# Reordering the side jobs and operand loads of an MLP stage in a fused hybrid block

## The reference

```
h   = modulate(x);  proj = h @ w_in                    # one wide projection
mix = gates * (fourier(proj) @ w_fp, hgrn(proj) @ w_hp) @ w_out + b_out
x   = layernorm(alpha * x + g1 * mix)
h2  = modulate(x)
x   = layernorm(alpha * x + g2 * (square(relu(h2 @ w1 + b1)) @ w2 + b2))    # w1: 1024 x 4096, w2: 4096 x 1024
```

## Time and profile before

| | |
|---|---|
| median of 3 runs | 3273.69 us (3273.14 to 3278.31) |
| the profiled execution | 3274.81 us, of which the span is 3273.0 us |
| mean granted TensorE clock | 0.957 of full speed |
| PE busy | 2954.5 us (90% of the span) |
| DVE busy | 1805.7 us (55%) |
| ACT busy | 1034.5 us (32%) |
| POOL busy | 681.8 us (21%) |
| up stage | 1802.8 us to about 2580 us of the span |
| down stage | from 2580.88 us to the end |

### The profile page before, as it was taken

How to read it: one execution, slowest core, us unless ns; L and a number is a source line. 1 busy time by engine, 2 the same in 40 slices (tenths; PEclk the granted TensorE clock), 3 DMA queues, 4 the chain that set the end, 5 groups by cost and what they waited for, 6 DMA issues and landing times.

```text
span 3273.0 us, 35996 instructions
## 1 busy us (share of the span) xinstructions
PE 2954.5 (90%) x13816; PEld 2425.4 (74%) x13816; DVE 1805.7 (55%) x2454; ACT 1034.5 (32%) x1676; POOL 681.8 (21%) x670
## 2 busy tenths in 40 slices
PE   6999999999996899989999788867999699989994
PEld 3888888888884688868788576756777588868883
DVE  5821133121223888677667666656666555586557
ACT  2421000111113565532112544435454433313330
POOL 0322011000001222112105011110000044464443
PEclk9999999999998999989999899988999899999997
DMA  6732233333325554468747687885766655545542
GB/s 227 256 105 81 78 103 126 107 123 124 103 104 171 160 169 154 126 181 215 229 158 257 235 249 235 251 247 181 222 198 193 209 194 187 212 161 206 194 179 96
DMA packets 332911, 573.00 MB, mean 175 GB/s; under 512 B 23731, under 2 KB 212419, under 8 KB 326726
## 3 DMA queue, kind: packets, MB, share of 16 engines
q1 hardware_dynamic: 256646, 330.00, 31.5%
q0 software_dynamic: 58128, 200.85, 18.2%
q10 hardware_dynamic: 17968, 39.85, 3.6%
HBM read 371.37 MB, written 199.24 MB: 174 GB/s over the span
## 4 chain that ended last, share of the span: by engine, by line
PE 48%; DVE 7%; DMA 6%; issue 3%; ACT 2%; POOL 1%; SPq 0%; ACTq 0%; DVEq 0%; POOLq 0%
PE mix_bank L1553 6%; PE mix_bank L1554 5%; PE mix_bank L1555 5%; PE mix_bank L1515 5%; PE mix_bank L1516 5%; PE mix_bank L1517 5%; PE mix_bank L2323 3%; PE mix_bank L2262 2%; PE mix_bank L130 2%; PE mix_bank L132 2%; PE mix_bank L131 2%; PE mix_bank L1460 1%; PE mix_bank L1461 1%; PE mix_bank L1462 1%; DMA tail_a<-scratch_a 1%
## 5 line engine op out<-in xcount | busy, mean ns | idle before, releaser
L1515 PE MATMUL mix_bank<-tail_oph,tail_wh 128*128 128x512 f32 x896 | 361.5, 403 | 124.1 <-ACT tail_e L1357 94.3
L130 PE MATMUL head_bank<-head_hTh,head_wh 128*128 128x512 f32 x1024 | 401.6, 392 | 2.9 <-DVE head_hTl L547 2.1
L131 PE MATMUL head_bank<-head_hTl,head_wh 128*128 128x512 f32 x1024 | 399.2, 390 | 0.0
L132 PE MATMUL head_bank<-head_hTh,head_wl 128*128 128x512 f32 x1024 | 399.1, 390 | 0.0
L1553 PE MATMUL mix_bank<-tail_oph,tail_ah 128*128 128x512 f32 x896 | 354.2, 395 | 45.4 <-issue 16.5
L1516 PE MATMUL mix_bank<-tail_opl,tail_wh 128*128 128x512 f32 x896 | 358.3, 400 | 0.0
L1517 PE MATMUL mix_bank<-tail_oph,tail_wl 128*128 128x512 f32 x896 | 357.3, 399 | 0.0
L1554 PE MATMUL mix_bank<-tail_opl,tail_ah 128*128 128x512 f32 x896 | 353.2, 394 | 0.0
L1555 PE MATMUL mix_bank<-tail_oph,tail_al 128*128 128x512 f32 x896 | 352.6, 394 | 0.0
L555 DVE CAST head_wh<-head_raw 128x1024 fp32r<-128x1024 f32 x64 | 44.1, 689 | 549.7 <-PE head_bank L132 414.6
L1151 DVE TENSOR_TENSOR tail_al<-tail_a,tail_ah 128x1024 fp32r<-128x1024 f32 x112 | 197.8, 1766 | 230.9 <-ACT tail_ah L1363 230.7
(11 more groups left out here) (275 smaller groups left out, 5548.8 us busy)
## 6 DMA issues: line engine op xcount, KB each, us to landing
tail_a<-scratch_a SPq DMA_DIRECT2D x112, 512.0 KB, 3.2
head_raw<-in_w_in SPq DMA_DIRECT2D x64, 512.0 KB, 4.1
scratch_proj<-head_stage POOLq DMA_DIRECT2D x128, 256.0 KB, 2.7
tail_raw<-in_w SPq DMA_DIRECT2D x64, 512.0 KB, 5.5
scratch_a<-tail_e SPq DMA_DIRECT2D x128, 256.0 KB, 4.9
tail_op<-scratch_w2t SPq DMA_DIRECT2D x28, 1024.0 KB, 5.6
scratch_a<-tail_sm SPq DMA_DIRECT2D x96, 256.0 KB, 8.5
tail_op<-in_w SPq DMA_DIRECT2D x21, 1024.0 KB, 6.0
```

The lines of the kernel that those rows point to most:

```text
L130: nc.tensor.matmul(out, wh, xh, start=(k == 0), stop=False)
L131: nc.tensor.matmul(out, wh, xl, start=False, stop=False)
L132: last = nc.tensor.matmul(out, wl, xh, start=False, stop=(k == k_tiles - 1))
L1515: nc.tensor.matmul(out[:], wh[p % 7][:, k, :], oph[i][:, k, :], start=(k == 0 and i in (0, 1, 3)), stop=False, skip_group_check=True)
```

## The change

Five edits, all in `tail_programs`:

1. The side jobs are in another order: the 16 row jobs first, then the 20 block sums.
2. They have other places (`WORK_AT`): two row jobs in each of the units 2 to 9, one behind product 1 and one behind product 5; one block sum behind product 5 in units 10 to 13; block sums behind products 1 and 5 in unit 14; none in 15 and 16; one behind product 5 in units 17 to 30. No turn has two jobs. The semaphore counts (`steps`, `mix_in`, `keep_left`, `store_left`, `load_row`, `load_mix`) follow.
3. First seam, SP: `load_h(1, 6)` stands ahead of the raw weights of unit 18 and of `store_mixed(15)`.
4. Second seam, SP: `load_a(0)`, `load_a(1)` and `load_w2(0, 0)`, `load_w2(0, 1)` stand ahead of `store_mixed(30)`; `load_a(0)` waits in addition for the stores of the last block sum.
5. Operand splits: `high_op(1, n)` and `low_op(1, n)` come four turns behind the product and not three; `high_op(2, 0)`, `low_op(2, 0)` and `high_op(2, 1)`, `low_op(2, 1)`, which stood behind turn 221, come inside the loop at turns 219 and 221, ahead of the splits of `a`.

```diff
-    WORK = list(range(4, MIX + NTILE))
-    FREE = [u for u in range(1, NU - 1) if u not in (UH - 1, UH)]
-
-    def jobs(u):
-
-        n = FREE.index(u) if u in FREE else None
-        return [] if n is None else WORK[n * len(WORK) // len(FREE):(n + 1) * len(WORK) // len(FREE)]
+    SPLIT = 2
+    WORK = [("row", n) for n in range(NTILE)] + [("mix", q) for q in range(4, MIX)]
+    SLOTS = [(u, i) for u in range(SPLIT, SPLIT + NTILE // 2) for i in (1, 5)] + [(u, 5) for u in range(10, UH - 1)] + [(UH - 2, 1)] + [
+        (u, 5) for u in range(UH + 1, NU - 1)]
+    WORK_AT = dict(zip(sorted(SLOTS), WORK))
+
+    def steps(q):
+        return 4 * q + (2 * NTILE if q >= 4 else 0)
...
             if r == 0:
                 sp.wait_ge(st_left, LEFT0 + 16 * NTILE)
+                sp.wait_ge(*mix_out(MIX - 1))
...
+            if u == UH:
+                sp.wait_ge(up_s, up_at[u - 1, 6] + 1)
+                load_h(1, 6)
             if u + 2 < NU:
                 sp.wait_ge(w_lo, up_at[u, 6] + 1)
                 load_raw(u + 2)
             if seam:
                 sp.wait_ge(up_s, up_at[u, 1] + 1)
                 load_h(1, 1)
+            if u == NU - 1:
+                load_a(0)
+                load_a(1)
+                for i in range(2):
+                    sp.wait_ge(up_s, up_at[u, i] + 1)
+                    load_w2(0, i)
             if u:
                 store_mixed(u - 1)
-            if u == UH:
-                sp.wait_ge(up_s, up_at[u - 1, 6] + 1)
-                load_h(1, 6)
...
             if u == NU - 1:
-                load_a(0)
-                load_a(1)
-                for i in range(4):
+                for i in (2, 3):
                     sp.wait_ge(up_s, up_at[u, i] + 1)
                     load_w2(0, i)
-                    if i in (1, 3):
-                        load_a(2 + i // 3)
+                    load_a(i)
...
-            if (u, i) != (UH - 1, 0) and p - 3 >= 0:
-                w, n = up_order[p - 3]
+            if p >= 4:
+                w, n = up_order[p - 4]
                 if w == UH - 1:
                     low_op(1, n)
...
-            if i == 5:
-                for x in jobs(u):
-                    mix(x) if x < MIX else keep_left(x - MIX)
+            if (u, i) in WORK_AT:
+                kind, n = WORK_AT[u, i]
+                mix(n) if kind == "mix" else keep_left(n)
...
             if p >= SEAM - LOOK2:
+                if p != SEAM - 2:
+                    low_op(2, (p + LOOK2 - SEAM) // 2)
                 low_a(p - (SEAM - LOOK2))
-        low_op(2, 0)
-        low_op(2, 1)
         down_turn(0)
...
             if n == 0:
-                pool.wait_ge(*mix_out(MIX - 1))
+                pool.wait_ge(*mix_out(2))
+                pool.wait_ge(z_s, NTILE)
+                for s in range(2):
+                    pool.wait_ge(st_hf[s], 16 * 4 * 4)
```

More of the change, by code:

```diff
@@ L780, in mix_in @@
     def mix_in(q):
-        return (ld_cm[q % 2], 32 * (q // 2 + 1)) if q < 4 else (ld_cm[0], 32 * (q - 1))
+        return (ld_cm[q % 2], 32 * (q // 2 + 1)) if q < 4 else (ld_cm[0], 64 + 32 + 16 * NTILE + 32 * (q - 3))
     def stored(n):
         return [(st_e[z], 16 * 7 * len(range(z, n, 3))) for z in range(3)]
-    WORK = list(range(4, MIX + NTILE))
-    FREE = [u for u in range(1, NU - 1) if u not in (UH - 1, UH)]
-    def jobs(u):
-        n = FREE.index(u) if u in FREE else None
-        return [] if n is None else WORK[n * len(WORK) // len(FREE):(n + 1) * len(WORK) // len(FREE)]
+    SPLIT = 2
[5 more added lines that the diff above has]
+        return 4 * q + (2 * NTILE if q >= 4 else 0)
     def kept_rows(t, n):
@@ L1136, in mix @@
             nc.vector.tensor_tensor(t[:, 0], b12, b11, ALU.subtract).then_inc(mix_s, 1)
-            dve.wait_ge(mix_s, 4 * q + 1)
+            dve.wait_ge(mix_s, steps(q) + 1)
             nc.vector.tensor_tensor(b12, b22, b12, ALU.subtract).then_inc(mix_s, 1)
             nc.vector.tensor_tensor(t[:, 1], b22, t[:, 0], ALU.subtract).then_inc(mix_s, 1)
-            dve.wait_ge(mix_s, 4 * q + 3)
+            dve.wait_ge(mix_s, steps(q) + 3)
             nc.vector.tensor_tensor(b21, b21, t[:, 1], ALU.subtract).then_inc(mix_s, 1)
         def keep_left(n):
-            dve.wait_ge(ld_cm[0], 32 * (MIX - 2) + 32 + 16 * (n + 1))
+            dve.wait_ge(ld_cm[0], 64 + 32 + 16 * (n + 1))
             nc.vector.tensor_tensor(cm[0][:, 0, :], cm[0][:, 0, :], cm[0][:, 1, :], ALU.mult).then_inc(mix_s, 1)
-            dve.wait_ge(mix_s, 4 * MIX + 2 * n + 1)
+            dve.wait_ge(mix_s, 16 + 2 * n + 1)
             nc.vector.tensor_tensor(cm[0][:, 0, :], cm[0][:, 0, :], ag[:], ALU.add).then_inc(mix_s, 1)
@@ L1417, in up_turn @@
                 high_op(0, 5 + p)
-            if p >= 3:
-                w, n = up_order[p - 3]
+            if p >= 4:
+                w, n = up_order[p - 4]
                 if w == UH - 1:
@@ L1436, in scalar @@
             if p >= SEAM - LOOK2:
+                if p != SEAM - 2:
+                    high_op(2, (p + LOOK2 - SEAM) // 2)
                 high_a(p - (SEAM - LOOK2))
-        high_op(2, 0)
-        high_op(2, 1)
         down_turn(0)
@@ L1586, in load_mix @@
             if q >= 2:
-                pool.wait_ge(*mix_out(q - 2 if q < 5 else q - 1))
+                pool.wait_ge(*(mix_out(q - 2) if q < 4 else (st_left, LEFT0 + 16 * NTILE) if q == 4 else mix_out(q - 1)))
             if q < 8:
@@ L1604, in store_mix @@
             dst = d["h2t"][q // 4, :, :, q % 4] if q < 8 else d["w2t"][(q - 8) // 4, :, :, q % 4]
-            pool.wait_ge(mix_s, 4 * q + 3)
+            pool.wait_ge(mix_s, steps(q) + 3)
             pool.dma_start(dst[0:2].rearrange("o p n -> p o n"), t).then_inc(mix_out(q)[0], 16)
-            pool.wait_ge(mix_s, 4 * q + 4)
+            pool.wait_ge(mix_s, steps(q) + 4)
             pool.dma_start(dst[2:4].rearrange("o p n -> p o n"), cm[b][:].rearrange("p i n -> p (i n)")[:, 512:1536].rearrange("p (o n) -> p o n", o=2)
@@ L1636, in store_left @@
         def store_left(n):
-            pool.wait_ge(mix_s, 4 * MIX + 2 * n + 2)
+            pool.wait_ge(mix_s, 16 + 2 * n + 2)
             pool.dma_start(d["xn1"][n * P:(n + 1) * P, :], cm[0][:, 0, :]).then_inc(st_left, 16)
@@ L1681, in gpsimd @@
                 mix(3)
[L1682 to L1685, removed]
-            else:
-                load_row(x - MIX)
-                store_left(x - MIX)
+        for kind, n in WORK:
+            if kind == "mix":
+                load_mix(n)
+                store_mix(n)
+            else:
+                load_row(n)
+                store_left(n)
         for v in range(1, NV):
```

## The result

The changed kernel takes 3228.71 us (median of 4 runs, 3221.51 to 3232.42), beside 3274.05 us for the one before on the same chip. The ratio is 0.9856 (95% interval 0.9837 to 0.9876): 47 us gained by the ratio and 45 between the medians, where 86 were forecast. The stated range ends at 3228 us: the median lies 0.7 us above it, and 3273.7 us times the ratio, 3226.6 us, lies just inside. The profiled execution took 3232.42 us (span 3230.6), 3.7 us over the median.

A forecast was written before the change was run, and what follows sets the result against it. PE, busy for 90% of the span, was taken as the bound, so time could come only from its pauses. Gains 67.6 - 15 + 23.3 + 10 = 85.9 us took 3273.7 to 3188 us; range 3160 to 3228 us.

The forecast's parts named there:

- part 1: Units 4, 7, 11, 20, 23 and 27: without a second job in a turn DVE doesn't wait; gain 67.6 us.
- part 2: Units 2 to 9, two rows each: DVE comes late at the closely spaced row pairs; cost 15 us, bounds 0 and 52.
- 7 such pairs: Row behind product 5 and the next behind product 1 of unit u+1, two turns apart; first costs 2.7 us.
- each later one costs about 2.05 us: Row pairs after the first: PE's delay lets the next job begin nearer to its product; 6 x 2.05 us.
- no half clock: Row pairs in units 2 to 9: PE's short pauses leave the clock up, as after one earlier 3.36 us pause.
- pairs drop the clock: Rival: each row pair stops PE for 5 us and half clock follows; 52 instead of 15 us, 3225 us; chance 0.15.
- part 3: Unit 14 and first seam: new loss 11 + 17 = 28 us instead of 51.3, gain 23.3 us.
- The sign given for the seam: First seam: the three units from 15 on would take some 75 us.
- The first seam's splits: First seam, seven operands split in ten turns: PE 14.6 us late, with half clock 17 us; bounds 4.5 and 33.
- part 4: Second seam: 12 us lost instead of 24.0, third down product may wait 2 us; gain 10 us, bounds 0 and 20.
- The slower rival: Row chain c in the seven tight gaps outgrows them; slower above c = 16.9 us, 3282 us at 18; chance 0.04.
- The other rivals: Rows hidden and seam short, 3165 us (0.15); seam loads share, not overtake, 3211 us (0.10); no effect, 3274 us (0.02).

The follow-up runs named there:

- e10: e8 with jobs at turns given one by one: rows four or five turns apart, block sums six, none in the first seam; 3223.14 us, ratio 0.9841.
- e11: Changed kernel with SP's seven stores (1.75 MB) held back in units 2 to 9 until the row behind product 5 has landed; 3221.66 us, ratio 0.9833.
- e3: Changed kernel with DVE leaving out the scaling and shifting of all 16 rows, POOL still loading and storing them; 3184.26 us (one run).
- e8: e7 with block sum 4 moved to (1, 5), ahead of the rows, so that unit 14 has one block sum; 3208.18 us, ratio 0.9809.
- e7: Changed kernel with row jobs behind products 4 and 6 instead of 1 and 5; 3218.55 us, ratio 0.9834.
- e6: e5 with block sum 4 moved to (1, 5), so that unit 14 has one job; 3209.64 us, ratio 0.9794.
- e9: e8 with load_h(1, 0), (1, 1), (1, 2) together in SP's unit 15, ahead of raw weights and sums; 3207.95 us, ratio 0.9795.
- e2: Kernel before the change with only the seams' loads and operand splits changed, without the wait of load_a(0); 3258.63 us, ratio 0.9961.
- e12: e10 with block sums seven turns apart and rows three or four turns apart; 3201.22 us, ratio 0.9789.
- e5: Changed kernel with each row job cut into two 256 KB halves using the buffer's halves by turns, behind products 1, 4, 0, 6; 3213.81 us, ratio 0.9808.

## Why the prediction came out as it did

- **The doubles (part 1)** are right to the last digit: the window over units 18 to 30 gives 247.52 us, 13 x 19.04, and DVE waits before the single block sums only once, for 0.80 us. A margin of 1 to 5 us was enough at one job in seven turns; e10, at six turns, shows how near that was, with gaps of up to 19 us between two block sums that end in a wait.
- **The rows (part 2)** are the step that failed. It said "7 such pairs" and "each later one costs about 2.05 us", 15 us, "with no half clock". Its wait of 3.7 us behind product 1 was measured at 3.69 to 3.99 in five of the six units 4 to 9, and at 5.20 in the other. But it counted only one of the two chains of a unit. Product 5 comes five turns behind product 1, 13.6 us, which leaves 11.1 beside the row's own 2.45, and I took for granted that a 7.00 us chain fits in. With the low part behind the row releasing SP's transfers, that chain is 14 to 15 us. DVE then waits twice a unit, PE pauses 4.6 to 5.1 us in five of the seven units instead of 2, and the half clock follows all but one of the pauses: 49.3 us. The inference "no half clock" from a single row of 3.36 us failed with it. This is the rival "pairs drop the clock" in manner and size (52 us, 3225 us, and units of 26 us as its sign); its counter-argument, that SP's raw loads go out behind the row, points at the cause: what SP sends there, the raw weights and above all the seven stores behind them, lands on the row's own store and load. e11 shows that SP's stores make the long chain, e3 that the loss comes through DVE alone, e10 that the rows cost 15 us where both chains have more room.
- **Unit 14 (part 3)** took 11 us for the first job, from a wait of 8.43 us (row below), and "waits little" for the second one. That waited 8.06 us: its chain is 2190.15 - 2172.09 = 18.1 us, again with SP's raw weights (issued at 2172.72) and the stores behind them in it, beside 11.6 us for the first. e8 puts the pair at 95.63 (e7) - 82.38 = 13 us, e6 at 15. The sign given for the seam, 75 us for three units, left out this pair, whose pause falls into unit 15; the sum itself implies 85, and 96.75 were measured.

```profile
2169.34 0.69 DVE L1141 TENSOR_TENSOR all_mod<-tail_cm 128x512 f32<-128x512 f32 x1 [8.43 <-DMA tail_cm<-in_w]
...
2190.15 0.69 DVE L1141 TENSOR_TENSOR all_mod<-tail_cm 128x512 f32<-128x512 f32 x1 [8.06 <-DMA tail_cm<-in_w]
```

- **The first seam's splits (part 3)** were forecast at 17 us; units 16 and 17 lose 12.9 and 10.6 us, 23.5 together. ACT's wait for `load_h(1, 6)`, 12.53 us in the earlier trace rows, is gone as forecast, and what is late next is partly DVE, as said. What I left out is `load_h(1, 2)`: it stays behind `store_mixed`, and ACT waits 4.06 us for it. e9, which moves it, leaves that undecided, so what the remaining loss hangs on stays open.

```profile
2217.74 1.90 ACT L1325 CAST tail_oph<-tail_op 128x2048 fp32r<-128x2048 f32 x1 [4.06 <-DMA tail_op<-scratch_h2t]
```

- **The second seam (part 4)**: forecast 12 us lost and 2 later, measured 7.6 and 4.8: 12.4 us, right in sum, by two errors of 4 and 3 us, which is luck. The later loss was forecast at the third down product, for data that comes late. It is at the fifth one, and not new: PE waits 9.88 us for DVE there, whose list the low parts of the operands fill, and waited 7.93 us in the kernel before (row below). The rest is a pause of 0.71 us and 2.1 us of PE's own time at the lower clock.

```profile
2618.04 0.77 PE L1553 MATMUL mix_bank<-tail_oph,tail_ah 128*128 128x512 f32 x1 [7.93 <-DVE tail_sum L1174]
```

- **The slower rival** needed c = 16.9 us in the tight gaps. The tight chains stayed at 6.8 to 8.3; it was the wide ones that grew, to 14 or 15.
- **The other rivals** fell: the rows were not hidden, and the seams' edits did gain (e2), loads and splits together.

A second buffer for the jobs, which would take the chains apart, was not tried. The causes of part 2 are shown. That the sum of chains gives the 24.5 us units of e7 follows from how chains are measured and is no separate proof. Why e12's rows lose 42 us at 3.8 turns stays open in detail.

## What to carry to other kernels

When jobs share one buffer, list every chain between them round the whole period and not only the shortest gap: where all are waited for, the period is their sum and the jobs' own work. Ask of each job what the instruction right behind it releases, since a burst that it lets go lands on the job's own store and load. A chain measured in a quiet place is its lower bound only; take the price with the neighbours' traffic in it before calling a gap wide enough.

## What the runs showed of the hardware

- A 512 KB row load took 3.3 us with nothing beside it (2007.86 to 2011.20), 3.8 us with 1 MB of raw weights issued 3.9 us earlier (e11), and 9.2 to 10.5 us beside the raw weights and SP's seven stores, 1.75 MB. Moving these stores behind the load took 6 to 7 us off it and its store, and put 3 us on the next row's store.
- The length of a PE pause alone did not decide the clock behind it. In the changed kernel a pause of 2.50 us left it at the upper of its two levels, and one of 2.28 us was followed by the lower one (first matmul 0.76 us). In e5 a pause of 4.16 us still left it at the upper one (0.47 us), while in the changed kernel all of 4.57 us and more were followed by the lower. e10's units 4 to 10, with six pauses of 0.5 to 2.6 us, had a granted clock of 1.00.
